# Head sums of both token halves as four quadrant products in the RWKV feature stage

## The reference

```
kk = k * k_k
k_mod = k * (1.0 + (a - 1.0) * k_a)
heads = lambda t: t.reshape(bsz, seq, H, N)             # 8 heads of 64
rh, kh, vh, wh, ah, kkh = map(heads, (r, k_mod, v, w, a, kk))
kkh = kkh / jnp.maximum(jnp.sqrt(jnp.sum(kkh * kkh, axis=-1, keepdims=True)), 1e-12)
...
bonus = (jnp.sum(rh * kh * r_k, axis=-1, keepdims=True) * vh).reshape(bsz, seq, W)
```

## Time and profile before

| what | us |
|---|---|
| median of the timed runs | 2864.79 |
| the profiled execution's own time | 2850.7 |
| its span | 2848.9 |
| TensorE busy in the span | 2725.7 (96%) |
| VectorE busy | 1876.4 (66%) |
| ScalarE busy | 1327.7 (47%) |
| the feature stage's tiles, first to last matmul record | about 1262 to 1642 |
| first and last `sums` product | 1337.7 and 1458.0 |

### The profile page before, as it was taken

One profiled execution on the slowest core, in us unless ns is written; L12 is line 12 of the kernel. 1 busy time (PEld: TensorE's weight loads), 2 busy tenths in 40 slices (PEclk: granted clock), 3 DMA queues, 4 the chain that ended last, 5 costly groups with the idle time before them and its releaser, 6 DMA issues. The chain is left out here.

```text
span 2848.9 us, 42015 instructions
## 1 busy us (share of the span) xinstructions
PE 2725.7 (96%) x16814; PEld 2143.3 (75%) x16814; DVE 1876.4 (66%) x2843; ACT 1327.7 (47%) x1932; POOL 271.0 (10%) x429
## 2 busy tenths in 40 slices
PE   7999989999999999989999998989899999999998
PEld 4757644777888888867778887777778888888886
DVE  6678987567666466784777516665755476656676
ACT  4247756467555334453441104542324565543344
POOL 0115630001000000000000001210000110000000
PEclk9999999999999999999999999999999999999999
DMA  7721100446566888722463332207233666677884
GB/s 265 227 69 38 49 1 1 141 151 239 208 236 215 300 282 293 247 93 62 127 155 125 124 118 78 81 29 227 84 98 130 222 218 225 221 290 259 291 286 151
DMA packets 205906, 474.01 MB, mean 166 GB/s; under 512 B 49040, under 2 KB 69648, under 8 KB 199376
## 3 DMA queue, kind: packets, MB, share of 16 engines
q1 hardware_dynamic: 187792, 393.73, 41.7%
q0 software_dynamic: 17920, 77.61, 6.9%
HBM read 344.09 MB, written 124.29 MB: 164 GB/s over the span
## 5 line engine op out<-in xcount | busy, mean ns | idle before, releaser
L2126 PE MATMUL psum<-merged_operand 128*128 128x512 f32 x1536 | 360.7, 390 | 0.0
L2126 PEld LDWEIGHTS psum<-merged_operand 128*128 128x128 f32 x1536 | 288.4, 188 | 60.7
L2126 PE MATMUL psum<-h_half_operand 128*128 128x512 f32 x1344 | 316.8, 391 | 0.0
L2126 PEld LDWEIGHTS psum<-h_half_operand 128*128 128x128 f32 x1344 | 252.3, 188 | 55.5 <-issue 1.0
L2126 PE MATMUL psum<-h_half_operand,weight_parts_operand 128*128 128x512 f32 x768 | 177.4, 392 | 0.8 <-DVE weight_parts_operand L2615 0.6
L2126 PEld LDWEIGHTS psum<-h_half_operand,weight_parts_operand 128*128 128x128 f32 x768 | 143.5, 188 | 34.1 <-DVE weight_parts_operand L2615 2.7
L3573 PE MATMUL psum<-h_high,weight_high 128*128 128x512 f32 x480 | 151.8, 397 | 1.4 <-DVE h_low L228 1.4
L3573 PE MATMUL psum<-h_low,weight_high 128*128 128x512 f32 x480 | 148.1, 390 | 0.0
L3573 PE MATMUL psum<-h_high,weight_low 128*128 128x512 f32 x480 | 147.9, 389 | 0.0
L215 DVE CAST weight_high<-weight_ring 128x1024 fp32r<-128x1024 f32 (+1 forms) x54 | 31.7, 586 | 164.7 <-PE psum L3573 105.4
L2615 DVE TENSOR_TENSOR weight_parts_operand<-weight_ring,weight_parts_operand 128x1024 fp32r<-128x1024 f32 x66 | 80.7, 1223 | 85.0 <-ACT weight_parts_operand L2275 84.6
(11 more groups left out here) (645 smaller groups left out, 5935.0 us busy)
## 6 DMA issues: line engine op xcount, KB each, us to landing
o<-in_w_ff SPq DMA_DIRECT2D x80, 512.0 KB, 4.5
merged<-hidden_terms SPq DMA_DIRECT2D x56, 512.0 KB, 5.7
hidden_upper<-in_w_ff_down SPq DMA_DIRECT2D x48, 512.0 KB, 4.9
weight_ring<-in_w_out SPq DMA_DIRECT2D x32, 512.0 KB, 3.4
hidden_terms<-weight_parts POOLq DMA_DIRECT2D x16, 1024.0 KB, 7.9
hidden_terms<-weight_ring POOLq DMA_DIRECT2D x16, 1024.0 KB
hidden_upper<-in_w_ff_up SPq DMA_DIRECT2D x32, 512.0 KB, 4.6
o<-hidden_terms SPq DMA_DIRECT2D x28, 512.0 KB, 5.8
```

The costliest lines, as they stand in the source:

```text
L2126: mm = pe.matmul(bank, w[:, at:at + P], tiles(r, i), start=opens and m == 0, stop=closes and m == 2, skip_group_check=resumed)
```

## The change

`sums` and `bonus_sums` no longer take a token half as an argument. Each is one group of four products behind one wait. A product takes 64 rows (one head) of one token half and a 64x64 block of `head_ones`, and writes 64 partitions of a bank. The bank follows the head (6 for the even one, 7 for the odd), and the half of the partitions is that of the head for g = 0 and the other one for g = 1 (`odd ^ g`). So the four products fill the four quadrants of the array. The group waits for the event of g = 1, where before each product waited for its own.

On VectorE the guard and the bonus multiply are made for 64 partitions at a time, so there are four of each for a head pair where there were two. For g = 1 an instruction reads PSUM in one half of the partitions and writes the other. The waits on ScalarE name the new events.

```diff
-        PE_EVENTS += [("rates", j, 0), ("rates", j, 1), ("sums", j, 0), ("sums", j, 1), ("bonus", j, 0), ("bonus", j, 1)]
+        PE_EVENTS += [("rates", j, 0), ("rates", j, 1), ("sums", j), ("bonus", j)]
...
+        def of_heads(odd):
+            return slice(odd * HD, (odd + 1) * HD)
+
+        def sums_of(g, odd):
+            return psum[of_heads(odd ^ g), 6 + odd, :]
...
                 def guard(j, g):
-                    dve.wait_ge(pe_sem, pe_at["sums", j, g])
-                    done(("guard", j, g), dve.tensor_scalar(norm[:, g, :], psum[:, 6 + g, :], 1e-24, None, op0=ALU.max))
+                    dve.wait_ge(pe_sem, pe_at["sums", j])
+                    for odd in range(2):
+                        done(("guard", j, g, odd), dve.tensor_scalar(norm[of_heads(odd), g, :], sums_of(g, odd), 1e-24, None,
+                                                                     op0=ALU.max))
...
-                    dve.wait_ge(pe_sem, pe_at["bonus", j, g])
-                    done(("bonus", j, g), dve.tensor_tensor(out=bonus[:, j, at(g)], in0=psum[:, 6 + g, :], in1=v,
-                                                            op=ALU.mult))
+                    dve.wait_ge(pe_sem, pe_at["bonus", j])
+                    for odd in range(2):
+                        done(("bonus", j, g, odd), dve.tensor_tensor(out=bonus[of_heads(odd), j, at(g)], in0=sums_of(g, odd),
+                                                                     in1=v[of_heads(odd)], op=ALU.mult))
...
-                def sums(j, g):
-                    pe.wait_ge(act_sem, act_at["square", j, g])
+                def sums_by_quadrant(of):
+                    for g in range(2):
+                        for odd in range(2):
+                            rows = of_heads(odd)
+                            mm = pe.matmul(sums_of(g, odd), K.const("head_ones")[rows, rows], of[rows, g, :], start=True, stop=True)
+                    c.step(mm)
+
+                def sums(j):
+                    pe.wait_ge(act_sem, act_at["square", j, 1])
                     if j:
-                        pe.wait_ge(dve_sem, dve_at["bonus", j - 1, g])
-                    c.step(pe.matmul(psum[:, 6 + g, :], K.const("head_ones"), norm[:, g, :], start=True, stop=True))
-
-                def bonus_sums(j, g):
-                    pe.wait_ge(dve_sem, dve_at["rk", j, g])
-                    c.step(pe.matmul(psum[:, 6 + g, :], K.const("head_ones"), e0[:, g, :], start=True, stop=True))
+                        pe.wait_ge(dve_sem, dve_at["bonus", j - 1, 1, 1])
+                    sums_by_quadrant(norm)
+
+                def bonus_sums(j):
+                    pe.wait_ge(dve_sem, dve_at["rk", j, 1])
+                    sums_by_quadrant(e0)
...
-                            act.wait_ge(dve_sem, dve_at["bonus", j, 1])
+                            act.wait_ge(dve_sem, dve_at["bonus", j, 1, 1])
...
-                        act.wait_ge(pe_sem, pe_at["bonus", j - 1, g])
+                        act.wait_ge(pe_sem, pe_at["bonus", j - 1])
...
-                        act.wait_ge(dve_sem, dve_at["guard", j, g])
+                        act.wait_ge(dve_sem, dve_at["guard", j, g, 1])
```

More of the change, by code:

```diff
@@ L3088, in shift_and_features @@
         DVE_EVENTS += [(e, j, g) for g in range(2) for e in ("kk", "a_less", "k_mod", "run", "before")]
-        DVE_EVENTS += [("guard", j, 0), ("guard", j, 1)]
+        DVE_EVENTS += [("guard", j, g, odd) for g in range(2) for odd in range(2)]
         DVE_EVENTS += [(e, j, g) for g in range(2) for e in ("unit", "b", "alpha", "rk", "rho", "beta", "kappa")]
-        DVE_EVENTS += [(e, j, g) for g in range(2) for e in ("beta_end", "kappa_end", "bonus")]
+        DVE_EVENTS += [e for g in range(2) for e in (("beta_end", j, g), ("kappa_end", j, g), ("bonus", j, g, 0), ("bonus", j, g, 1))]
     ACT_EVENTS += ["dt", "sin", "cos", "half", "exp_small"]
@@ L3634, in _ @@
                     if 1 <= j <= WT and i == 0:
-                        bonus_sums(j - 1, 0)
-                        bonus_sums(j - 1, 1)
+                        bonus_sums(j - 1)
                     if n >= 3 and j < WT:
@@ L3644, in _ @@
                         if i == 2:
-                            sums(j, 0)
-                            sums(j, 1)
+                            sums(j)
             @block.scalar
@@ L3670, in keep @@
                                 act.wait_ge(early[g].sem, early0[g] + EARLY * (WT - 1))
-                            act.wait_ge(dve_sem, dve_at["bonus", WT - 2, 1])
+                            act.wait_ge(dve_sem, dve_at["bonus", WT - 2, 1, 1])
                         else:
```

## The result

The changed kernel takes 2864.41 us (median of 20 runs, 2858.38 to 2876.31), beside 2859.36 us for the kernel before in runs on the same chips (20 runs, 2850.27 to 2865.03). The ratio is 1.0026, with a 95% interval of 1.0016 to 1.0036: slower by 7.4 us, between 4.6 and 10.3. (The two medians alone are 5.05 us apart; the ratio is estimated from all the runs.) The forecast was 2876.2 us, slower by 11.4, in a range of 2868.5 to 2884. The time is 11.8 us under the forecast and 4.1 under the range. The direction is right. Of the 11.8 us, 5.4 lie in the base, which was 2864.79 against 2859.36 here, and 6.4 in the difference of the medians, 5.05 against 11.4.

The account below looks back on a forecast made before the run. The prediction took TensorE to bound the changed stage, except its waits for VectorE's `rk`. Late `rk` (5.8 us) plus clock falls (5.6) made 11.4 us, giving 2876.2 us, range 2868.5 to 2884.

Parts of the forecast that it names:

- The sums save 0.48 us: Sums of squares on TensorE: four quadrant products save 0.48 us per head pair, which doesn't bring the guard forward.
- Four quadrants run together: TensorE's new groups: four products run at once, 0.86 us of streaming per group; rival, quadrants apart, chance 0.05.
- Two more guards, 1.45 us, on the chain: VectorE, between sums and Ln: half guards cost as much as whole ones, so `rk` ends 1.45 us later per head pair.
- Crossed reads: VectorE's reads across partition halves: nothing extra taken, upper bound 0.59 us each; rival, dear crossing, 4.7 us more, chance 0.05.
- The wait of 3.47 us: TensorE before the bonus sums: idle 3.47 us instead of 0.68, waiting for the second `rk`, in each head pair.
- The slack behind the bonus multiplies: VectorE's 3.91 us idle time after them: 1.45 us of extra multiplies leave 2.4 us, so they cost nothing.
- The clock falls, 1.4 us each: TensorE's clock halves after each long wait for `rk`: 4 x 1.4 = 5.6 us; rival, no fall, +5.8 total, chance 0.12.
- all six have the fall behind them: TensorE in the trace before: all six waits over 2.6 us precede a clock fall, so 3.47 us would too.
- The sum of 11.4 us: Whole kernel: 5.8 us of waits plus 5.6 us of clock falls make it 11.4 us slower; forecast chance 0.70.
- the last one: From profile to timed runs: their median is 14.1 us above the profiled execution; the same 11.4 added gives 2876.2 us.

Follow-up runs that it names:

- The guards alone: The kernel before with each guard made in two instructions of 64 rows, no quadrant product and no crossed read: ratio 1.0032, stage 310.9 us.
- the filled wait: The changed kernel with 14 small identity matmuls that nobody reads before each wait for the second `rk`: 2864.18 us, ratio 1.0025, stage 310.8 us.
- the second, 13.7: The changed kernel run once more, unaltered, for a second profiled execution and more timed runs: 2869.5 us, ratio 1.0048, stage 315.5 us.

## Why the prediction was wrong, and where it was right

- **The sums save 0.48 us.** The profile has 0.51. This was right, and so was that it doesn't reach the end.
- **Four quadrants run together.** The four products of a group are over within 1.09 us at full clock, in each kernel that has them. This was right.
- **Two more guards, 1.45 us, on the chain.** They take 1.44 in the profile and 5.8 us over four head pairs. The guards alone show it (310.9 against 305.1) and, with the clock taken out, so does the filled wait (310.8). This was right. Crossed reads cost nothing that can be seen, which is the bound that I took.
- **The wait of 3.47 us.** It measured 3.49. This was right.
- **The slack behind the bonus multiplies.** I forecast 2.4 us left of 3.91. With the filled waits, where the clock doesn't fall, VectorE's idle time there is 2.42; in the changed kernel's profile it is 3.94:

```profile
1368.19 0.69 DVE L215 CAST weight_high<-weight_ring 128x1024 fp32r<-128x1024 f32 x1 [2.42 <-PE psum L3582]
```

```profile
1366.38 0.69 DVE L215 CAST weight_high<-weight_ring 128x1024 fp32r<-128x1024 f32 x1 [3.94 <-PE psum L3582]
```

  In the second, TensorE's tile was itself late by its low clock, some 1.6 us, which gave the 1.45 back. The sum was right, and so was the conclusion that it costs nothing.
- **The clock falls, 1.4 us each.** In eight waits of 3.5 us it fell seven times, at about 1.6 us each. So the size was right within 0.2 us. The ground that I gave for it was too strong: "all six have the fall behind them", of waits over 2.6 us. The trace of before has five such waits, not six, and all five do have the fall; but in the later runs four waits of 2.62 to 2.69, one of 2.63 and one of 3.49 have none. The length of a wait alone doesn't decide it; what else does was not tried.
- **The sum of 11.4 us.** In the stage it is 12.0 and 10.3 in the two profiled executions, so the mechanism and its terms hold there. Against the comparison that was timed first, 7.4 (4.6 to 10.3), it is too high; against the second, 13.7 (8.9 to 18.8), it is not. Over all runs it is 9.6.
- **The step that failed is the last one**, from the stage to the timed runs: "The median of the timed runs is 14.1 higher, and I add the same 11.4 to it". Its base was mis-sized. The three runs behind it, 2863.01 to 2865.03, were at the top of what this kernel does (2846.65 to 2865.53 over all its runs, median 2858). The same kernel's median beside the result was 2859.36, 5.4 us lower, and the mean of its other runs is 7 us lower than that of the three. Had the base been 2859.36, the forecast would have been 2870.8 us, and a range as wide around it would have begun at 2863.1 and held the result. The other 6.4 us of the miss lie in the difference: the medians moved by 5.05 and not by 11.4. No term of the stage accounts for that. The stage itself measured 10.3 to 12.0, and over all runs the means moved by 9.6, so I take most of it for the scatter of executions, which is argued and not shown; some 2 us stay open.
- **What the range left out.** The profiled execution, 2850.7, was near the bottom, and I had both numbers before me: 14.1 us between executions of one program is larger than the effect to be forecast, and I put none of it in the range. It began at 2868.5, 4 us over the time.

## What to carry to other kernels

Half the partitions is not half the time on VectorE (0.69 us for 64x512 as for 128x512 here), so tiling a product into quadrants buys TensorE time with VectorE instructions: first see which engine waits for which. Where the other engine is waited for, take the operand that doesn't need the slow chain out of it; the same change then took 4.7 us off the stage, where it had added 12.0. And where a program's executions spread by more than the effect, forecast and judge by the length of the stage between two fixed marks, and widen the range of the total by the spread of its base.

## What the runs showed of the hardware that was not expected

The executions of one kernel differ by their time at half clock. In the changed kernel's 20 runs it goes from 80 us (in the run of 2858.38) to 121 us (in that of 2876.31), and the run times go with it, with a correlation of -0.92 between time and mean granted clock. Filling four waits of 3.5 us with products that nobody reads took 6.3 us off the stage in the profile, and 2.8 (0.5 to 5.2) off the mean of the timed runs. And in one execution four waits of 2.62 to 2.69 us between dense products kept the full clock, where a wait of 2.64 us at the end of the same stage lost it. That last wait is 2.63 or 2.64 us in all ten profiled executions; behind it the clock fell in nine of them and stayed at 1.00 in the one with the halved guards.
